# First FFN: eight modulation chunks through ScalarE and VectorE instead of TensorE

## The reference, cut to what matters

```python
for l in range(DEPTH):
    m_lat = split(silu(c)     @ ada_w[l] + ada_b[l], 6)    # six vectors of 1024: shift, scale, gate, twice
    m_ctx = split(silu(c_ctx) @ ada_w[l] + ada_b[l], 6)
    h_lat, h_ctx = modulate(x_lat, m_lat[0], m_lat[1]), modulate(x_ctx, m_ctx[0], m_ctx[1])
    ...                                                     # attention, layer norm, conv FFN
# conv_ffn: u = h @ w_up; three taps along the tokens; silu(g) * a; @ w_down
```

## Time and profile before

| | us |
|---|---|
| median of 3 runs | 1589.31 (1589.12 to 1590.01) |
| the profiled execution | 1588.72 |
| its span | 1587.3 |
| TensorE busy in the span | 1551.7 (98%) |
| VectorE busy | 1069.3 (67%) |
| ScalarE busy | 881.3 (56%) |
| GpSimd busy | 338.0 (21%) |

### The profile page before, as it was taken

How to read it: one execution, slowest core, us unless ns; L and a number is a source line. 1 busy time by engine, 2 the same in 40 slices (tenths; PEclk the granted TensorE clock), 3 DMA queues, 4 the chain that set the end, 5 groups by cost and what they waited for, 6 DMA issues and landing times.

```text
span 1587.3 us, 25560 instructions
## 1 busy us (share of the span) xinstructions
PE 1551.7 (98%) x9960; PEld 1325.5 (84%) x9960; DVE 1069.3 (67%) x1982; ACT 881.3 (56%) x1735; POOL 338.0 (21%) x335
## 2 busy tenths in 40 slices
PE   7999999999999999999999999999999999999998
PEld 4788778988887888978999988878888898788886
DVE  4834766665444435898787777777987667779874
ACT  2413973765653323577555545655766556567663
POOL 0201420455530000022011102232221013312210
PEclk9999999999999999999999999999999999999999
DMA  8767023354756324112456543324555443335552
GB/s 362 309 242 228 21 81 133 133 203 170 263 212 239 107 88 151 41 68 92 161 186 226 186 176 132 138 87 176 188 187 187 175 163 127 131 142 186 186 201 78
DMA packets 46951, 260.35 MB, mean 164 GB/s; under 512 B 11888, under 2 KB 13168, under 8 KB 18160
## 3 DMA queue, kind: packets, MB, share of 16 engines
q1 hardware_dynamic: 43952, 252.78, 43.9%
q0 software_dynamic: 1296, 4.72, 0.9%
q10 hardware_dynamic: 1584, 1.23, 0.2%
HBM read 257.64 MB, written 1.07 MB: 163 GB/s over the span
## 4 chain that ended last, share of the span: by engine, by line
PE 89%; DVE 5%; ACT 3%; DMA 1%; issue 1%; POOL 0%; DVEq 0%; ACTq 0%
PE ps L512 22%; PE ps L513 21%; PE ps L514 21%; PE ps L764 8%; PE ps L765 5%; PE ps L667 2%; PE ps L689 2%; PE ps L676 2%; PE ps L528 2%; PE ps L766 1%; DMA raw<-in_ada 1%; PE ps L1164 1%; PE ps L575 1%; ACT arena L1826 1%; ACT wh L1435 1%
## 5 line engine op out<-in xcount | busy, mean ns | idle before, releaser
L1925 DVE TENSOR_TENSOR wl<-raw,wh 128x1024 fp32r<-128x1024 f32 (+2 forms) x308 | 362.2, 1217 | 249.3 <-ACT wh L1435 248.1
L1435 ACT CAST wh<-raw 128x1024 fp32r<-128x1024 f32 (+1 forms) x318 | 313.6, 1036 | 326.7 <-PE ps L514 294.1
L512 PE MATMUL ps<-xx,wh 128*128 128x256 f32 (+1 forms) x1006 | 328.3, 326 | 3.3 <-DVE wl L1931 3.2
L514 PE MATMUL ps<-xx,wl 128*128 128x256 f32 (+1 forms) x1006 | 325.4, 323 | 0.0
L513 PE MATMUL ps<-xx,wh 128*128 128x256 f32 (+1 forms) x1006 | 325.4, 323 | 0.0
L512 PE MATMUL ps<-wh,xx 128*128 128x512 f32 (+2 forms) x780 | 286.4, 367 | 1.9 <-issue 0.8
L513 PE MATMUL ps<-wl,xx 128*128 128x512 f32 (+2 forms) x780 | 281.3, 361 | 0.0
L514 PE MATMUL ps<-wh,xx 128*128 128x512 f32 (+2 forms) x780 | 281.2, 361 | 0.0
L2296 DVE SCALAR_TENSOR_TENSOR arena<-ps,pv,arena 128x254 f32<-128x254 f32 (+2 forms) x352 | 193.0, 548 | 28.7 <-ACT arena L1637 19.3
L512 PEld LDWEIGHTS ps<-xx,wh 128*128 128x128 f32 x1006 | 191.2, 190 | 24.0 <-ACT wh L1435 4.0
L514 PEld LDWEIGHTS ps<-xx,wl 128*128 128x128 f32 x1006 | 191.2, 190 | 15.1
(11 more groups left out here) (242 smaller groups left out, 2241.4 us busy)
## 6 DMA issues: line engine op xcount, KB each, us to landing
raw<-in_ada SPq DMA_DIRECT2D x46, 1024.0 KB, 5.2
raw<-in_up SPq DMA_DIRECT2D x44, 1024.0 KB, 4.9
raw<-in_fin SPq DMA_DIRECT2D x44, 1024.0 KB, 4.8
raw<-in_down SPq DMA_DIRECT2D x22, 1024.0 KB, 4.8
raw<-in_fout SPq DMA_DIRECT2D x22, 1024.0 KB, 4.8
raw<-in_win SPq DMA_DIRECT2D x12, 1024.0 KB, 4.9
raw<-in_ev_w_in SPq DMA_DIRECT2D x9, 1024.0 KB, 8.1
raw<-in_wout SPq DMA_DIRECT2D x8, 1024.0 KB, 4.8
```

Of the source, the lines that this page charges most:

```text
L512: e.matmul(out, A[0], B[0], start=first, stop=False)
L514: return e.matmul(out, A[1], B[0], start=False, stop=last)
L1435: e.copy(hi_of(j)[:, a:b], raw_of(j)[:, a:b]).then_inc(*S.hi.up((j, half)))
L1925: e.tensor_tensor(lo_of(j)[:, a:b], raw_of(j)[:, a:b], hi_of(j)[:, a:b].bitcast(F), ALU.subtract).then_inc(*S.lo.up((j, half)))
```

## The change

The eight chunks for both conditions no longer go to TensorE as they are. Each is loaded with the chunk order's steps 5 to 18 and handled in one step of `BOTH_AT` (3, 5, 8, 10, 11, 13, 14, 16). ScalarE begins two accumulators of 128x256 (one a condition) with a product each, VectorE adds the other seven products to each: fourteen multiply-adds, alternating between the two, each waiting for the one before the last. The accumulators of two chunks lie in `tmp` and in a part of `arena` that is free, in turn. TensorE sums two chunks at a time over the partitions with four matmuls (`both_sums`) in steps 10, 14 and 18 (two times). The latent chunks' sums move a step later (6, 10, 14, 18), and the finish of all from step 18 to 19, with four transposes instead of two; the selection matmuls go.

```diff
-ADA_AT = {17: [(6, 0), (6, 1)], 18: [(6, 2), (6, 3), (6, 4)], 19: [(6, 5), (6, 6), (6, 7)]}
-FINISH_AT = {20: 6}
+BOTH_AT = {3: 0, 5: 1, 8: 2, 10: 3, 11: 4, 13: 5, 14: 6, 16: 7}
+BOTH_SUM_AT = {10: (0,), 14: (1,), 18: (2, 3)}
-SUM_AT = {5: 0, 9: 1, 13: 2, 17: 3}
-SUM_FINISH = 18
+SUM_AT = {6: 0, 10: 1, 14: 2, 18: 3}
+SUM_FINISH = 19
 # chunk_order, in step f
-        o += ada(1, *[i for g, i in ADA_AT.get(f - 1, ())])
+        if f - 2 in BOTH_AT:
+            o.append(("ada1", BOTH_AT[f - 2], CH, "both"))
+    ADA_BOTH = AR(13312, 4, 256)
+    def both_place(b):
+        return ADA_BOTH if b % 2 else tmp4
 # TensorE
+        def both_sums(j):
+            if j == 0:
+                wait_bank(6)
+            q.wait_ge(*S.both.at(2 * j + 1))
+            for g in range(4):
+                m = e.matmul(ps[6][32 * g:32 * g + 32, 0:256], onep[:, 3 - j:35 - j], both_place(j)[:, g, :],
+                             start=j == 0, stop=j == 3)
+            m.then_inc(*S.ada.up(("bothsums", j)))
...
-                        for n_, i in ADA_AT.get(f, ()):
-                            ada(n_, i)
                         if f in SUM_AT:
                             ada_sums(SUM_AT[f])
+                        for n_ in BOTH_SUM_AT.get(f, ()):
+                            both_sums(n_)
...
-                if ada_every and f in FINISH_AT:
-                    ada_finish(FINISH_AT[f])
 # ScalarE, at the end of a step, behind ada_products
+        def ada_begin(i):
+            j, (b, n) = J["ada1", i], divmod(i, 2)
+            q.wait_ge(*S.raw[SLOT[j]].at(j))
+            if b >= 2:
+                q.wait_ge(*S.ada.at(("bothsums", b - 2)))
+            elif b == 1:
+                q.wait_ge(*S.affine.at((0, 0, 2)))
+            for v in range(2):
+                e.mul(both_place(b)[:, 2 * n + v, :], raw_of(j)[:, 0:256], sil[:, 0, v:v + 1]).then_inc(*S.act.up(("begun", i, v)))
 # VectorE, at the end of a step, behind the affine
+        def ada_both(i):
+            j, n = J["ada1", i], i % 2
+            wv = raw_of(j).rearrange("p (k n) -> p k n", k=8)
+            q.wait_ge(*S.raw[SLOT[j]].at(j))
+            for k in range(1, 8):
+                for v in range(2):
+                    acc = both_place(i // 2)[:, 2 * n + v, :]
+                    q.wait_ge(*(S.act.at(("begun", i, v)) if k == 1 else S.both.at((i, v, k - 1))))
+                    e.scalar_tensor_tensor(acc, wv[:, k, :], sil[:, k, v:v + 1], acc, ALU.mult, ALU.add).then_inc(
+                        *S.both.up((i, v, k), *([i] if (k, v) == (7, 1) else [])))
 # SyncE, before a load into the slot of such a chunk
+                elif before[3] == "both":
+                    q.wait_ge(*S.both.at(before[1]))
```

More of the change, by code:

```diff
@@ L69 @@
 GROUPS = [[(0, c), (0, c + 4)] for c in range(4)] + [[(0, 8 + c) for c in range(8)], [(0, 16 + c) for c in range(8)]]
-GROUPS += [[(1, c) for c in range(8)]]
-ADA_AT = {17: [(6, 0), (6, 1)], 18: [(6, 2), (6, 3), (6, 4)], 19: [(6, 5), (6, 6), (6, 7)]}
-FINISH_AT = {20: 6}
+BOTH_AT = {3: 0, 5: 1, 8: 2, 10: 3, 11: 4, 13: 5, 14: 6, 16: 7}
+BOTH_SUM_AT = {10: (0,), 14: (1,), 18: (2, 3)}
 NSUM = 16
-SUM_AT = {5: 0, 9: 1, 13: 2, 17: 3}
-SUM_FINISH = 18
+SUM_AT = {6: 0, 10: 1, 14: 2, 18: 3}
+SUM_FINISH = 19
 LATER = (2, 2, 2, 2, 2, 2, 2, 2)
@@ L84 @@
     "hi", "ea", "xh", "exp", "act",
-    "lo", "ev", "xl", "vec", "mods", "conv",
+    "lo", "ev", "xl", "vec", "mods", "conv", "both",
     "lop", "gps", "prod", "affine",
@@ L95, in __init__ @@
          self.hi, self.ea, self.xh, self.exp, self.act,
-         self.lo, self.ev, self.xl, self.vec, self.mods, self.conv,
+         self.lo, self.ev, self.xl, self.vec, self.mods, self.conv, self.both,
          self.lop, self.gps, self.prod, self.affine) = self.all = [
@@ L545, in ada_sums @@
                 free[7] = [(S.vec, "sumrows")]
+        def both_sums(j):
[6 more added lines that the diff above has]
+            m.then_inc(*S.ada.up(("bothsums", j)))
+            if j == 3:
+                free[6] = [(S.vec, "sumrows")]
         def sums_finish():
             q.wait_ge(*S.vec.at("sumrows"))
-            for f in range(2):
-                m = e.transpose(ps[7][:, 128 * f:128 * f + 128], adat[:, 1, 128 * f:128 * f + 128], ident)
+            for b in range(2):
+                for f in range(2):
+                    m = e.transpose(ps[6 + b][:, 128 * f:128 * f + 128], adat[:, b, 128 * f:128 * f + 128], ident)
             m.then_inc(*S.adat.up("sums"))
-            free[7] = [(S.mods, "sums")]
+            free[6] = free[7] = [(S.mods, "sums")]
         def ada_finish(n):
@@ L1642, in ffn @@
                     ada_products(8 + f)
+                if ada_every and f in BOTH_AT:
+                    ada_begin(BOTH_AT[f])
             gate(NT - 1)
@@ L1960, in sum_rows @@
         def sum_rows():
-            q.wait_ge(*S.ada.at(("sums", 3)))
-            e.tensor_copy(adat[:, 1, :], ps[7][:, 0:256]).then_inc(*S.vec.up("sumrows"))
+            q.wait_ge(*S.ada.at(("bothsums", 3)))
+            for b in range(2):
+                e.tensor_copy(adat[:, b, :], ps[6 + b][:, 0:256]).then_inc(*S.vec.up("sumrows"))
         def sum_mods():
@@ L1970, in sum_mods @@
                 e.tensor_tensor(dst[:, f, :, :], src[:, f, :, :], b[:, f, :, :], ALU.add).then_inc(*S.mods.up("sums"))
+            src = ps[6][:, 0:256].rearrange("p (f n v r) -> p f n v r", f=2, n=2, v=2)[:, :, :, :, 0:4]
+            dst = mods[:, 1, 0:16, :].rearrange("p (j n f) v -> p f n v j", j=4, n=2)
+            b = vec("ada_b", 48, 16).rearrange("p (j n f) -> p f n j", j=4, n=2)
+            for f in range(2):
+                for n in range(2):
+                    e.tensor_tensor(dst[:, f, n, :, :], src[:, f, n, :, :], b[:, f, n, :].unsqueeze(1).broadcast_to([128, 2, 4]),
+                                    ALU.add).then_inc(*S.mods.up("sums"))
+        def ada_both(i):
[8 more added lines that the diff above has]
+                        *S.both.up((i, v, k), *([i] if (k, v) == (7, 1) else [])))
         def low(key, k):
@@ L2273, in ffn @@
             for f in range(NT):
-                if ada_every and f - 1 in FINISH_AT:
-                    ada_mods(FINISH_AT[f - 1])
                 if ada_every and f - 1 == SUM_FINISH:
@@ L2301, in ffn @@
                     next(spare, None)
-                if ada_every and f + 1 in FINISH_AT:
-                    ada_rows(FINISH_AT[f + 1])
+                if ada_every and f in BOTH_AT:
+                    ada_both(BOTH_AT[f])
                 if ada_every and f + 1 == SUM_FINISH:
```

## The result

| | before | after |
|---|---|---|
| median of the runs | 1588.40 us (1587.30 to 1590.01) | 1592.35 us (1586.12 to 1596.39) |
| ratio to before | | 1.0019, 95% interval 1.0011 to 1.0027 |
| the profiled execution | 1588.72, span 1587.3 | 1587.07, span 1585.6 |

The change costs 3.0 us by the ratio and 3.95 by the medians. That is about half or less of the 7.3 that were forecast, and inside the forecast's range. The executions of the changed kernel lie ten us apart, those of before three.

A forecast was written before the change was run, and what follows sets the result against it. TensorE, busy 98% of the span, was taken to bound the kernel. Waits of 13.4 us for VectorE's weights less a gain of 6.1 made it 7.3 us slower, forecast 1596.5 us (8 in 10: 1583 to 1608).

The forecast's parts named there:

- TensorE's gain: Work removed from steps 17 to 19 and the chain, 8.02 us, less 1.94 added: 6.1 us net.
- ScalarE, DMA, the end: Added products hidden in ScalarE's idle time, moved loads in time, later sums not waited for: no cost.
- Own price of a multiply-add: Each added 256-wide multiply-add on VectorE takes 0.397 us from start to start, 5.56 us a chunk.
- VectorE held by GpSimd: Steps 3 to 16: GpSimd's turns hold VectorE 4.7 us per chunk step, 1.7 per plain step, 47.8 together.
- whoever waits gets the next turn: VectorE and GpSimd instructions with two SBUF operands take strict turns, one instruction at a time.
- 28 is the least: Lower bound in us for holding over fourteen steps, if every turn falls well; then nothing waits, gain 6.1.
- The multiply-adds of step 3: First added step: fourteen multiply-adds of 5.56 us, held 4.7 by GpSimd's adds and product, ending at 17.9.
- The sum over steps 3 to 16: VectorE's own work 128.5 plus held 47.8, less 155.6 at hand and 7.3 allowed lateness: TensorE waits 13.4 us.
- rival A: VectorE keeps up in steps 3 to 16, held under 34.4 us, TensorE never waits: 1583.2 us; chance 0.21.
- rival B: Stall and gain cancel, VectorE held 37 to 44 us over steps 3 to 16: 1586 to 1592.5; chance 0.12.

The follow-up runs named there:

- quiet: The changed kernel with GpSimd's first two adds of each latent chunk 4 columns wide, multiply-adds whole; 1583.17 us, ratio 0.9968.
- narrow: The changed kernel with its 112 multiply-adds 8 columns wide instead of 256; 1583.28 us, ratio 0.9967.
- late2: As late, with all sums but the last pair's one step later on TensorE; 1581.99 us, ratio 0.9959.
- a1: The changed kernel, unaltered, run and profiled again; 1592.85 us, ratio 1.0025.
- a2: The changed kernel, unaltered, profiled once more; 1594.91 us (one execution).
- late: The changed kernel with chunks in steps 4, 8, 10, 12, 14, 16, 17, 18, fourth sum and finish in step 20; 1586.66 us, ratio 0.9983.

## Why the prediction was wrong

*TensorE's gain, right.* Forecast 6.1, measured 6.12 from the casts; 5.1 and 5.2 by the ratios of quiet and narrow, 6.5 (4.4 to 8.7) by late2. The casts that start at the ends of steps 3 and 21 frame the steps of TensorE that the change touches:

| run | end of step 3 | end of step 21 | between |
|---|---|---|---|
| before | 316.61 | 524.03 | 207.42 |
| narrow | 317.23 | 518.53 | 201.30 |
| quiet | 316.77 | 518.07 | 201.30 |
| the changed kernel, first profile | 316.78 | 521.90 | 205.12 |
| a1 | 317.19 | 529.07 | 211.88 |
| a2 | 318.99 | 530.87 | 211.88 |

Without waits it takes 201.30, which is 6.12 less than before.

*ScalarE, DMA, the end, right.* No wait of TensorE in the first FFN ends there (where a row names ScalarE's cast, the low weights come last, as above), and narrow, which keeps all of them, has the whole 6.12.

*Own price of a multiply-add, right.* 0.397 from start to start where GpSimd is still.

*The step that failed: VectorE held by GpSimd.* It said "whoever waits gets the next turn", and so 4.7 us in each step with a chunk, 1.7 in each without, 47.8 in all, and "28 is the least". Measured: 32.4, 36.3 and 36.7. The multiply-adds of step 3, worked out, were right to 0.1 us (10.34; forecast 5.56 + 4.7). The next line of the same working was not: GpSimd's next add was to get its turn between the two halves of the weights, which would be done at 22.5, and TensorE was to wait 0.7 us. The add was passed over, the weights were done at 20.7, and TensorE did not wait. I then used step 3 for all eight, though from step 5 on VectorE is late and meets GpSimd elsewhere: with the convolution, with the product, or not at all (step 16, where GpSimd has no adds left, 1.0 to 1.2). And GpSimd's request is often passed over until VectorE's run of two-source instructions ends. The trace of before has no such run longer than three in its first FFN, so it could not show this; I took its turns for a rule.

*The sum over steps 3 to 16.* It pooled lateness: 128.5 + 36.5 - 155.6 - 7.3 would be waits of 2.1 us; a1 and a2 have 6.83 and 6.86, and the first execution has 1.94 with 32.4 held, where the sum gives none. The bounds of rival A fell with it: no wait with less than 34.4 us held, and a gain up to 40.5; a1 and a2 have 36.3 and 36.7, and are 4.5 us slower in the first FFN. A wait comes from the worst few steps in a row, and idle time elsewhere (some 2 to 4 us before the weights) doesn't pay for it.

*A missing term: the clock.* Each of the five waits in the three executions cost another 1.9 us (a2's step 8: 15.85 less 10.88 less 3.10). With it the first FFN adds up: 201.30 + 1.94 + 1.89 = 205.13 in the first execution (205.12), and 201.30 + 6.86 + 2 x 1.87 = 211.90 in a2 (211.88). Whole spans don't compare that closely: a2 is 1.8 us behind a1 already at the end of step 3, and the clock behind the 2.21 us wait at 955 to 975 us adds some 1.2 us in some executions and not in others.

So waits of 13.4 us were forecast and 1.9 to 6.9 came, with 1.9 to 3.8 of the clock on top. For a1 and a2 the errors are these: 11.3 too much held, 4.7 of waits that the pooled sum can't see, 3.8 of the clock. The last two make good 8.5 of the 11.3. With the holding measured and nothing else mended, the sum would have given 2.1 of waits and a kernel 4 us faster; that the direction came out right is luck. By its time, rival B was closest (1586 to 1592.5), though its mechanism, 37 to 44 us held with no other loss, was not what happened.

## What to carry to other kernels

Work that fits an idle engine on average still costs where it bunches: count the lateness over the worst few steps in a row, then spread the added work, and put each consumer of its result a step further back than the mean suggests (late2: one step, some 4 us by the two ratios, 1.9 of them seen in the traces). When the bottleneck is TensorE, price a wait of about 2 us at up to twice its length: here waits of 1.94 to 3.84 us cost up to 1.9 more, though one of 2.47 and four of the ten of 2.21 didn't. A shared resource read from one pattern of the trace (single instructions in turn) need not behave so in another (a run of them back to back).

## What the runs showed of the hardware

VectorE and GpSimd with two SBUF sources each: in the profiles of the changed kernel, a1, a2, late and late2 there are 41 GpSimd adds and products that asked while an unheld multiply-add ran, counted from single instructions. Of the 8 that came within 0.05 us of its start all were passed over; of the 22 at 0.09 to 0.32 us 18 got the turn at once (0.03 to 0.24 us of waiting); of the 11 at 0.36 us and later all were passed over, by one instruction to seven. Those passed over waited 0.3 to 4.9 us, most until VectorE's run ended. Where VectorE had itself been held, the turns alternated. The Trainium skill (SBUF — State Buffer, Who interferes with whom) has the first comer hold the pair for its whole instruction; that agrees with what holds VectorE (step 3: fourteen multiply-adds in 10.34 us instead of 5.63). The same section has "Issue order, not op shape, decides who blocks." By the starts that the traces record this doesn't hold for 23 of the 41 requests: instructions of VectorE that started after them, up to eight in a row, went first. The measurement decides.
